# The feed-forward stage of a four-layer model: all remainders made by VectorE, another order of the first and last splits, and other PSUM banks for the last token tile

## The chip, the cores and the metric

The kernel runs on one core of one Trainium2 chip. The metric is the time of one execution in device microseconds. The kernel before took 2660.16 us (median of 3 runs, 2657.3 to 2661.0).

## The reference

The program computes two layers of one kind (attention, two recurrent mixers, a mixture of experts) and then two layers of a second kind. The change is in the last stage of the second kind, which runs twice, once in each of those two layers (sequence 512, D_MODEL 1024, D_FF 2816):

```python
x = x + mix @ w_out[l]

h2 = rms_norm(x, ffn_norm_g[l])
x = x + (jax.nn.silu(h2 @ w_gate[l]) * (h2 @ w_up[l])) @ w_down[l]
```

Everything is fp32.

## The kernel before

The whole stage is `out_ffn_stage`. It is called twice, with the same shapes.

**Products from parts.** TensorE multiplies fp32r values. Each operand is split into a rounded high part, written by ScalarE as a copy (`..._hi`), and a remainder `raw - hi`, written by VectorE or GpSimd as a subtraction (`..._lo`). `product` issues three matmuls for each tile: hi·hi, hi·lo, lo·hi (lines 233 to 235, in helper functions used everywhere).

**The output projection.** Four token tiles t of 128 rows; for each, two halves of 512 columns are summed in PSUM banks (`sum_bank`). VectorE adds them to x (`add`), ScalarE squares (`square`), VectorE normalises into `h` (`normalise`), and TensorE transposes `h` in eight blocks (`turn`, line 1956), four to each of two banks (`turn_bank`, banks 4 and 5). `turn(3)`, for the last tile, stands on TensorE behind the first two groups of the gate and up projections.

**Gate and up projection.** The product is done with seven half-size products P1 to P7 instead of eight (Strassen's scheme, in Winograd's form): for each of C = 11 chunks of 256 hidden columns, the seven products of `PRODUCTS` are *groups*, g = 0 to 76, each 24 matmuls of 256 columns. Groups 0 to 3 are P1 and P2 of chunks 0 and 1, 4 to 8 the rest of chunk 0, 9 to 13 the rest of chunk 1, and from 14 on seven for each chunk. The token operands (`x_operands`, names A11, A12, A22, S1 to S4) are made once: VectorE makes the sums S1 to S4 for the token tiles 2 and 3 (`make_sum`, lines 2172 to 2182), ScalarE their high parts (`split_sum`, line 2062; `split_a22`, line 2067), and GpSimd (line 2141) or VectorE (2187, 2192) the remainders. The weight operands are made for each group: VectorE makes the sums T3, T1, T2, T4 of a chunk (`make_w`, line 2214), ScalarE the high part (`w_split_hi`, line 1882), and `w_split_lo` (line 1888) the remainder. They lie in a ring of four places (RING = 4): the split of group g waits until group g - 4 has been multiplied.

**The order of work.** It is written out by hand, for each engine its own list; each engine goes through its list in order, and a semaphore holds it where an input or a place is not ready. In the middle, iteration g of ScalarE's and VectorE's loops does the split of group g and then `after(g - 4)`, which combines the products of a group into the hidden values: VectorE's lines 2223 to 2243, ScalarE's copy of P1 (2075) and its two Silus (2078 and 2081). A list `by_pool` says which engine makes a group's remainder: GpSimd for the first four groups and for P1, P7, P5 and P3, VectorE for P2, P6 and P4.

**Down projection.** The hidden values are split in eleven parts j (`hidden_split_hi`, line 2086; `hidden_split_lo`, line 1894). The high part of j overwrites token operands, so it waits for the last product that reads those (`hidden_free`). Twelve weight units of the down projection follow; the first (`ffn_down_hi`, `ffn_down_lo`) has places of its own, the others go through `weights_hi` and `weights_lo` (lines 208 and 222). A unit of the first half needs two hidden parts.

## Time and profile before

| | us |
|---|---|
| median of 3 runs | 2660.16 |
| profiled execution, its own time | 2654.06 |
| span of the profiled execution | 2651.9 |
| TensorE busy with matmuls | 2399.8 (90%) |
| VectorE busy | 1750.7 (66%) |
| ScalarE busy | 1313.7 (50%) |
| GpSimd busy | 906.0 (34%) |

Times in the trace are counted from the start of the span. The first run of the stage lies between 1506 and 1925 us, the second between 2229 and the end. A mean over the span says little about this stage: what counts is which wait of TensorE ends last at each place.

### The profile page before, as it was taken

The page shows a single profiled execution, that of the slowest core. Times are in us where ns is not written, and L with a number is a line of the kernel's source. Part 1 is how long each engine was busy: PE and PEld are TensorE (multiplying, and loading weights), DVE is VectorE, ACT ScalarE, POOL GpSimd, SP SyncE. Part 2 cuts the span into 40 slices and gives each one's busy share as a digit, 9 for nine tenths or more (in the row PEclk, how much of TensorE's full clock was granted, in tenths as well). Part 3 has the DMA queues.
Part 4 walks back from the last instruction along what each step waited for, and adds up shares of the span by engine and source line. Part 5 has one row for each costly group of instructions (what it writes and reads, how often), then busy time and mean ns, then how long its engine had stood idle before and what let it go on. Part 6 is the DMA issues. An engine that isn't in the chain of part 4 may idle for free. (4 is left out here: it accounts for less than half of the span.)

```text
span 2651.9 us, 37244 instructions
## 1 busy us (share of the span) xinstructions
PE 2399.8 (90%) x14216; PEld 2019.2 (76%) x14216; DVE 1750.7 (66%) x2637; ACT 1313.7 (50%) x2638; POOL 906.0 (34%) x447
## 2 busy tenths in 40 slices
PE   7999887977999887977998989998989989899989
PEld 7866676767866676767786779996877857899967
DVE  1855757863845757867698569884256984788832
ACT  3556616763546616755746644442157465444511
POOL 3401305762402205762350155551024401555510
PEclk9999888998999888998998999999999999999999
DMA  4200018973200108973220203322121202023211
GB/s 157 85 32 1 31 66 331 353 280 125 81 33 1 32 35 337 356 272 123 80 80 1 77 34 110 111 104 80 67 105 64 80 1 88 32 105 119 96 72 72
DMA packets 54992, 285.82 MB, mean 108 GB/s; under 512 B 13216, under 2 KB 13216, under 8 KB 28704
## 3 DMA queue, kind: packets, MB, share of 16 engines
q1 hardware_dynamic: 45600, 266.65, 27.5%
q0 software_dynamic: 9216, 16.80, 1.7%
q8 instruction: 114, 1.87, 0.3%
q14 instruction: 62, 0.51, 0.1%
HBM read 275.02 MB, written 25.17 MB: 113 GB/s over the span
## 5 line engine op out<-in xcount | busy, mean ns | idle before, releaser
L222 POOL TENSOR_TENSOR weights_lo<-weights_raw,weights_hi 128x2048 fp32r<-128x2048 f32 (+4 forms) x53 | 239.8, 4525 | 503.1 <-ACT weights_hi L208 335.7
L233 PE MATMUL ps<-x_operands,weights_hi 128*128 128x256 f32 x1232 | 351.9, 286 | 7.0 <-POOL weights_lo L1888 6.1
L234 PE MATMUL ps<-x_operands,weights_hi 128*128 128x256 f32 x1232 | 350.2, 284 | 0.0
L235 PE MATMUL ps<-x_operands,weights_lo 128*128 128x256 f32 x1232 | 347.6, 282 | 0.0
L208 ACT ACTIVATE weights_hi<-weights_raw 128x2048 fp32r<-128x2048 f32 (+5 forms) x86 | 147.9, 1722 | 306.3 <-PE ps L235 294.6
L233 PEld LDWEIGHTS ps<-x_operands,weights_hi 128*128 128x128 f32 x1232 | 233.1, 189 | 9.4 <-POOL weights_lo L1888 7.3
L235 PEld LDWEIGHTS ps<-x_operands,weights_lo 128*128 128x128 f32 x1232 | 236.0, 192 | 0.0
L234 PEld LDWEIGHTS ps<-x_operands,weights_hi 128*128 128x128 f32 x1232 | 233.5, 189 | 0.0
L233 PE MATMUL ps<-weights_hi,attn_ht_hi 128*128 128x512 f32 (+2 forms) x576 | 203.1, 353 | 8.3 <-DVE weights_lo L222 6.9
L235 PE MATMUL ps<-weights_hi,attn_ht_lo 128*128 128x512 f32 (+2 forms) x576 | 200.4, 348 | 0.0
L234 PE MATMUL ps<-weights_lo,attn_ht_hi 128*128 128x512 f32 (+2 forms) x576 | 200.0, 347 | 0.0
L222 DVE TENSOR_TENSOR weights_lo<-weights_raw,weights_hi 128x2048 fp32r<-128x2048 f32 (+3 forms) x33 | 65.0, 1973 | 188.6 <-ACT weights_hi L208 188.6
L233 PE MATMUL ps<-weights_hi,x_operands 128*128 128x512 f32 x384 | 155.2, 404 | 24.4 <-DVE weights_lo L222 18.1
L1882 ACT ACTIVATE weights_hi<-ffn_w_sums 128x1024 fp32r<-128x1024 f32 x66 | 69.9, 1059 | 191.4 <-DVE ffn_w_sums L2214 183.7
L1888 POOL TENSOR_TENSOR weights_lo<-weights_raw,weights_hi 128x1024 fp32r<-128x1024 f32 x50 | 128.2, 2566 | 82.3 <-ACT weights_hi L1882 82.0
L234 PE MATMUL ps<-weights_lo,x_operands 128*128 128x512 f32 x384 | 154.4, 402 | 0.0
L233 PE MATMUL ps<-weights_hi,xt_hi 128*128 128x480 f32 (+2 forms) x384 | 138.1, 360 | 6.1 <-DVE weights_lo L222 2.5
L235 PE MATMUL ps<-weights_hi,xt_lo 128*128 128x480 f32 (+2 forms) x384 | 135.3, 352 | 0.0
L234 PE MATMUL ps<-weights_lo,xt_hi 128*128 128x480 f32 (+2 forms) x384 | 134.9, 351 | 0.0
L233 PEld LDWEIGHTS ps<-weights_hi,attn_ht_hi 128*128 128x128 f32 x576 | 109.5, 190 | 31.7 <-issue 9.1
L235 PE MATMUL ps<-weights_hi,ffn_hidden_lo 128*128 128x512 f32 x320 | 126.9, 397 | 0.0
L235 PEld LDWEIGHTS ps<-weights_hi,attn_ht_lo 128*128 128x128 f32 x576 | 109.5, 190 | 12.7
(526 smaller groups left out, 6521.9 us busy)
## 6 DMA issues: line engine op xcount, KB each, us to landing
weights_raw<-in_stream SPq DMA_DIRECT2D x96, 1024.0 KB, 4.7
weights_raw<-in_expert_gu SPq DMA_DIRECT2D x34, 1024.0 KB, 9.1
expert_raw<-in_expert_gu SPq DMA_DIRECT2D x30, 1024.0 KB
expert_raw<-in_expert_down SPq DMA_DIRECT2D x18, 1024.0 KB, 8.0
weights_raw<-in_expert_down SPq DMA_DIRECT2D x14, 1024.0 KB
weights_raw<-in_stream SPq DMA_DIRECT2D x12, 960.0 KB, 4.6
ffn_raw<-in_stream SPq DMA_DIRECT2D x10, 1024.0 KB, 5.1
weights_raw<-in_stream SPq DMA_DIRECT2D x8, 700.0 KB, 9.9
```

What stands on the lines that cost most here:

```text
L208: self.nc.scalar.activation(self.split_tiles(u)[0][:, 0:n], self.env.raw[:, u % self.RAW, 0:n], ACT.Copy).then_inc(self.hi_ready, 1)
L222: eng.tensor_tensor(lo[:, 0:n], self.env.raw[:, u % self.RAW, 0:n], hi[:, 0:n].bitcast(F32), ALU.subtract).then_inc(self.lo_ready, 1)
L233: nc.tensor.matmul(out, a[0], b[0], start=start, stop=False, **more)
L234: nc.tensor.matmul(out, a[0], b[1], start=False, stop=False, **more)
L235: return nc.tensor.matmul(out, a[1], b[0], start=False, stop=stop, **more)
L1882: nc.scalar.activation(ring(g)[0], quarter(c, w_of[p]), ACT.Copy).then_inc(w_hi_done, 1)
L1888: eng.tensor_tensor(lo, quarter(c, w_of[p]), hi.bitcast(F32), ALU.subtract).then_inc(w_lo_pool if by_pool[g] else w_lo_dve, 1)
```

## The change

- `by_pool` is False for every group: VectorE (line 1891 in the new file) makes every weight remainder, and those of the token sums and of all hidden parts. GpSimd keeps only the four remainders of A11 and A12.
- The transposes of the last token tile go to banks 2 and 3 instead of 4 and 5 (`turn_bank(t, b)`), and the products take their banks from a table, `PRODUCT_BANKS`, instead of counting on from 6.
- VectorE makes the first T3, T1 and T2 behind `normalise(1)` instead of `normalise(2)`; the remainders of groups 0 to 3 stand before and just behind the last `add`.
- ScalarE splits all four first groups ahead of `square(3)`. The token parts are made in the order of a list, `TOKEN_PARTS`.
- The hidden parts are made in the order 0, 1, 6, 7, 8, 9, 4, 5, 2, 3, 10 (`HIDDEN_ORDER`). ScalarE makes ten high parts in one row behind the first down unit; VectorE puts two remainders ahead of each of the last `after` calls. Both engines put the second down unit ahead of hidden part 10.

```diff
+PRODUCT_BANKS = (6, 7, 0, 1, 4, 5, 2, 3)
+TOKEN_PARTS = (("S3", 2), ("S2", 2), ("A22", 2), ("S3", 3), ("S2", 3), ("S1", 2), ("S4", 2), ("S1", 3), ("S4", 3), ("A22", 3))
+HIDDEN_ORDER = (0, 1, 6, 7, 8, 9, 4, 5, 2, 3, 10)
...
-    by_pool = [g < RING or p in ("P1", "P7", "P5", "P3") for g, (_, p) in enumerate(order)]
+    by_pool = [False] * N
...
-        def turn_bank(b):
-            return ps[:, 4 + b, :].rearrange("p (k s) -> p k s", k=4)
+        def turn_bank(t, b):
+            return ps[:, (2 if t == T - 1 else 4) + b, :].rearrange("p (k s) -> p k s", k=4)
...
-            return ps[:, (at[c, p] + 6) % NBANK, :]
+            return ps[:, PRODUCT_BANKS[at[c, p] % NBANK], :]
...
@@ TensorE
-                        if t == 3:
-                            pe.wait_ge(s_made, s_at("S2" if b else "S3", 2))
-                            if b == 1:
-                                pe.wait_ge(s_hi, 5)
-                                pe.wait_ge(s_lo_dve, 1)
+                        if t == T - 1:
+                            pe.wait_ge(added, 2 * t + b + 1)
...
-                    if g < 6:
-                        pe.wait_ge(added, 6 if g < 4 else 8)
-                    elif g == 6:
-                        pe.wait_ge(s_made, s_at("S3", 3))
-                    elif g == 7:
-                        pe.wait_ge(s_made, s_at("S2", 3))
-                        pe.wait_ge(s_lo_dve, 6)
+                    if g < 4:
+                        pe.wait_ge(added, 6)
+                    elif g < NBANK:
+                        t = 2 + (g - 4) // 2
+                        pe.wait_ge(s_made, s_at("S2" if g % 2 else "S3", t))
+                        if g % 2:
+                            pe.wait_ge(s_lo, s_split("A22", t))
...
@@ ScalarE
-                w_split_hi(act, 0)
-                w_split_hi(act, 1)
+                for g in range(RING):
+                    w_split_hi(act, g)
                 square(3)
-                w_split_hi(act, 2)
                 split_sum("S3", 2)
                 split_sum("S2", 2)
-                w_split_hi(act, 3)
+                split_a22(2)
                 after(0)
+                w_split_hi(act, 4)
+                after(1)
+                w_split_hi(act, 5)
+                split_sum("S3", 3)
+                split_sum("S2", 3)
                 split_sum("S1", 2)
                 split_sum("S4", 2)
...
-                    after(g - RING)
                     if g == N:
...
                         stream.split_hi(act, down)
-                    if g >= N:
-                        for j in range(3 * (g - N), min(3 * (g - N) + 3, C - 1)):
+                        for j in HIDDEN_ORDER[:-1]:
                             hidden_split_hi(j)
-                hidden_split_hi(C - 1)
-                for u in range(down + 1, down + len(downs) + 2):
+                    after(g - RING)
+                stream.split_hi(act, down + 1)
+                hidden_split_hi(HIDDEN_ORDER[-1])
+                for u in range(down + 2, down + len(downs) + 2):
...
@@ VectorE
-                for m in ("T3", "T1", "T2"):
-                    make_w(0, m)
+                    if t == 1:
+                        for m in ("T3", "T1", "T2"):
+                            make_w(0, m)
                 add(3, 0)
+                for g in range(3):
+                    w_split_lo(v, g)
                 add(3, 1)
                 make_sum("S3", 2)
                 make_sum("S2", 2)
+                w_split_lo(v, 3)
                 normalise(3)
...
-                    after(g - RING)
                     if g == N:
...
                         stream.split_lo(v, down)
                     if g >= N:
-                        for j in range(3 * (g - N), min(3 * (g - N) + 3, C - 1)):
-                            if not hidden_by_pool[j]:
-                                hidden_split_lo(v, j)
-                if not hidden_by_pool[C - 1]:
-                    hidden_split_lo(v, C - 1)
+                        for j in HIDDEN_ORDER[2 * (g - N):2 * (g - N) + 2]:
+                            hidden_split_lo(v, j)
+                    after(g - RING)
+                for j in HIDDEN_ORDER[2 * RING:-1]:
+                    hidden_split_lo(v, j)
+                stream.split_lo(v, down + 1)
+                hidden_split_lo(v, HIDDEN_ORDER[-1])
```

Some lines of the new file are numbered otherwise than before: 1888 is 1891 (weight remainder), 1894 is 1897 (hidden remainder), 2172 to 2182 are 2156 to 2166 (token sums), 2187 and 2192 are 2172 (token remainders), 2214 is 2193 (weight sums), 2223 to 2243 are 2202 to 2222 (combining).

VectorE's order at the start of the stage, from the last token tile's sums to the weight remainder of group 5 (`ps` is PSUM, `ffn_sums` holds S1 to S4). Before:

```order
L2172 TENSOR_TENSOR ffn_sums<-ffn_parts,ps 128x512
L2176 TENSOR_TENSOR ffn_sums<-ps,ffn_sums 128x512
L2161 RECIPROCAL ffn_rs<-ffn_rs 128x1
L2164 SCALAR_TENSOR_TENSOR ffn_h<-x,ffn_rs,ffn_g 128x1024
L2179 TENSOR_TENSOR ffn_sums<-ffn_sums,ffn_parts 128x512
L2182 TENSOR_TENSOR ffn_sums<-ffn_a_15839,ffn_sums 128x512
L2192 TENSOR_TENSOR x_operands<-ps,x_operands 128x4x128
L2172 TENSOR_TENSOR ffn_sums<-ffn_parts,ps 128x512
L2176 TENSOR_TENSOR ffn_sums<-ps,ffn_sums 128x512
L2187 TENSOR_TENSOR x_operands<-ffn_sums,x_operands 128x4x128 x2
```

and now:

```order
L1891 TENSOR_TENSOR weights_lo<-weights_raw,weights_hi 128x1024
L2145 RECIPROCAL ffn_rs<-ffn_rs 128x1
L2148 SCALAR_TENSOR_TENSOR ffn_h<-x,ffn_rs,ffn_g 128x1024
L2163 TENSOR_TENSOR ffn_sums<-ffn_sums,ffn_parts 128x512
L2166 TENSOR_TENSOR ffn_sums<-ffn_a_15839,ffn_sums 128x512
L2172 TENSOR_TENSOR x_operands<-ffn_sums,x_operands 128x4x128 x2
L2172 TENSOR_TENSOR x_operands<-ps,x_operands 128x4x128
L2156 TENSOR_TENSOR ffn_sums<-ffn_parts,ps 128x512
L2160 TENSOR_TENSOR ffn_sums<-ps,ffn_sums 128x512
L1891 TENSOR_TENSOR weights_lo<-ffn_w_sums,weights_hi 128x1024
L2172 TENSOR_TENSOR x_operands<-ffn_sums,x_operands 128x4x128 x2
L1891 TENSOR_TENSOR weights_lo<-ffn_w_sums,weights_hi 128x1024
```

The remainders of the token sums and of groups 3, 4 and 5 now stand in VectorE's row, the one of A22 (`x_operands<-ps`) two places later.

VectorE's order at the end of the gate and up projection, from the first down unit on (`ffn_hidden_lo` are the hidden parts' remainders, the last rows the next down units). Before:

```order
L222 TENSOR_TENSOR ffn_down_lo<-weights_raw,ffn_down_hi 128x2048
L1894 TENSOR_TENSOR ffn_hidden_lo<-ffn_hidden,x_operands 128x1024 x2
L2232 TENSOR_TENSOR ffn_parts<-ffn_parts,ps 128x512
L2233 TENSOR_TENSOR ffn_parts<-ffn_parts,ps 128x512
L1894 TENSOR_TENSOR ffn_hidden_lo<-ffn_hidden,x_operands 128x1024
L2235 TENSOR_TENSOR ffn_hidden<-ffn_parts,ps 128x2x256
L1894 TENSOR_TENSOR ffn_hidden_lo<-ffn_hidden,x_operands 128x1024 x2
L2238 TENSOR_TENSOR ffn_parts<-ffn_parts,ps 128x512
L2241 TENSOR_TENSOR ffn_hidden<-ffn_hidden,ffn_parts 128x2x256
L2243 TENSOR_TENSOR ffn_hidden<-ffn_hidden,ffn_parts 128x2x256
L1894 TENSOR_TENSOR ffn_hidden_lo<-ffn_hidden,x_operands 128x1024
L222 TENSOR_TENSOR weights_lo<-weights_raw,weights_hi 128x2048 x4
```

and now, from the fourth row of it on:

```order
L2208 TENSOR_TENSOR ffn_parts<-ffn_parts,ps 128x512
L1897 TENSOR_TENSOR ffn_hidden_lo<-ffn_hidden,x_operands 128x1024 x2
L2211 TENSOR_TENSOR ffn_parts<-ffn_parts,ps 128x512
L2212 TENSOR_TENSOR ffn_parts<-ffn_parts,ps 128x512
L1897 TENSOR_TENSOR ffn_hidden_lo<-ffn_hidden,x_operands 128x1024 x2
L2214 TENSOR_TENSOR ffn_hidden<-ffn_parts,ps 128x2x256
L1897 TENSOR_TENSOR ffn_hidden_lo<-ffn_hidden,x_operands 128x1024 x2
L2217 TENSOR_TENSOR ffn_parts<-ffn_parts,ps 128x512
L2220 TENSOR_TENSOR ffn_hidden<-ffn_hidden,ffn_parts 128x2x256
L2222 TENSOR_TENSOR ffn_hidden<-ffn_hidden,ffn_parts 128x2x256
L1897 TENSOR_TENSOR ffn_hidden_lo<-ffn_hidden,x_operands 128x1024 x2
L222 TENSOR_TENSOR weights_lo<-weights_raw,weights_hi 128x2048
```

Eleven remainders instead of six stand in VectorE's row; two pairs of ten lie behind `after(75)` or later, and the second down unit now stands ahead of the eleventh.

## Rows read from the trace of the kernel before

**Rows 1.** Waits of TensorE, whole span: us in total, times, longest

```profile
PE ps L1956 <- DVE x_operands L2192: 9.2, 2, 4.6
...
PE ps L233 <- POOL weights_lo L1888: 6.1, 6, 1.9
```

**Rows 2.** Timeline of TensorE, start of the first stage: start, us, instruction, idle before

```profile
1556.27 0.36 PE L233 MATMUL ps<-x_operands,weights_hi 128*128 128x256 f32 x1 [0.30 <-PE ps L235]
...
1567.30 1.09 PE L1956 MATMUL ps<-consts,ffn_h 128*128 128x128 f32 x4 [4.61 <-DVE x_operands L2192]
1568.04 0.56 PE L233 MATMUL ps<-x_operands,weights_hi 128*128 128x256 f32 x1
...
1572.67 0.34 PE L233 MATMUL ps<-x_operands,weights_hi 128*128 128x256 f32 x1
...
1589.97 0.38 PE L233 MATMUL ps<-x_operands,weights_hi 128*128 128x256 f32 x1 [1.93 <-POOL weights_lo L1888]
...
1614.62 0.39 PE L233 MATMUL ps<-x_operands,weights_hi 128*128 128x256 f32 x1 [0.88 <-POOL weights_lo L1888]
```

**Rows 3.** Windows: us, busy us of PE, PEld, DVE, ACT, POOL, granted clock, DMA

```profile
1505.00:1510.00 5.00, 3.52 (x11) 2.89 (x12) 2.70 (x3) 3.48 (x2) 0.00 (x0) 0.79 0.86 313
...
1565.00:1570.00 5.00, 2.70 (x13) 2.73 (x14) 3.14 (x5) 3.08 (x6) 5.00 (x4) 0.60 0.00 0
```

**Rows 4.** Timeline of VectorE, start of the first stage

```profile
1559.64 2.89 DVE L2179 TENSOR_TENSOR ffn_sums<-ffn_sums,ffn_parts 128x512 f32<-128x512 f32 x1
...
1576.82 1.22 DVE L1888 TENSOR_TENSOR weights_lo<-ffn_w_sums,weights_hi 128x1024 fp32r<-128x1024 f32 x1
1577.96 0.68 DVE L2192 TENSOR_TENSOR x_operands<-ps,x_operands 128x512 fp32r<-128x512 f32 x1
1578.56 2.82 DVE L2214 TENSOR_TENSOR ffn_w_sums<-weights_raw,ffn_w_sums 128x1024 f32<-128x1024 f32 x1
```

**Rows 5.** Timeline of ScalarE at the first Silu of the first stage

```profile
1582.01 0.63 ACT L2078 ACTIVATE ffn_hidden<-ffn_hidden 128x512 f32<-128x512 f32 x1 [3.10 <-DVE ffn_hidden L2223]
1582.55 1.04 ACT L1882 ACTIVATE weights_hi<-ffn_w_sums 128x1024 fp32r<-128x1024 f32 x1
```

**Rows 6.** Timeline of VectorE, a late chunk and a weight sum of an early one

```profile
1619.27 1.21 DVE L2214 TENSOR_TENSOR ffn_w_sums<-weights_raw,ffn_w_sums 128x1024 f32<-128x1024 f32 x1
...
1778.30 1.21 DVE L2214 TENSOR_TENSOR ffn_w_sums<-weights_raw,ffn_w_sums 128x1024 f32<-128x1024 f32 x1
1780.69 1.23 DVE L1888 TENSOR_TENSOR weights_lo<-ffn_w_sums,weights_hi 128x1024 fp32r<-128x1024 f32 x1 [1.19 <-ACT weights_hi L1882]
```

**Rows 7.** Timeline of VectorE, end of the gate and up projection

```profile
1785.12 2.29 DVE L222 TENSOR_TENSOR ffn_down_lo<-weights_raw,ffn_down_hi 128x2048 fp32r<-128x2048 f32 x1 [1.29 <-ACT ffn_down_hi L208]
1787.33 6.78 DVE L1894 TENSOR_TENSOR ffn_hidden_lo<-ffn_hidden,x_operands 128x1024 fp32r<-128x1024 f32 x2
...
1809.04 4.49 DVE L222 TENSOR_TENSOR weights_lo<-weights_raw,weights_hi 128x2048 fp32r<-128x2048 f32 x2 [0.58 <-ACT weights_hi L208]
```

**Rows 8.** Timeline of GpSimd, same place

```profile
1786.96 16.14 POOL L1894 TENSOR_TENSOR ffn_hidden_lo<-ffn_hidden,x_operands 128x1024 fp32r<-128x1024 f32 x5 [2.78 <-ACT x_operands L2086]
```

**Rows 9.** Timeline of ScalarE, same place

```profile
1783.09 1.90 ACT L208 ACTIVATE ffn_down_hi<-weights_raw 128x2048 fp32r<-128x2048 f32 x1
1784.89 8.63 ACT L2086 ACTIVATE x_operands<-ffn_hidden 128x1024 fp32r<-128x1024 f32 x9
```

**Rows 10.** Timeline of TensorE, first and second down unit, first stage

```profile
1790.98 0.47 PE L233 MATMUL ps<-ffn_down_hi,x_operands 128*128 128x512 f32 x1 [0.42 <-DVE ffn_hidden_lo L1894]
...
1811.47 0.77 PE L233 MATMUL ps<-weights_hi,x_operands 128*128 128x512 f32 x1 [9.06 <-DVE weights_lo L222]
...
1815.31 0.39 PE L233 MATMUL ps<-weights_hi,x_operands 128*128 128x512 f32 x1
```

**Rows 11.** Timeline of TensorE, the same two places of the second stage

```profile
2290.90 1.09 PE L1956 MATMUL ps<-consts,ffn_h 128*128 128x128 f32 x4 [4.61 <-DVE x_operands L2192]
...
2535.09 0.77 PE L233 MATMUL ps<-weights_hi,x_operands 128*128 128x512 f32 x1 [9.07 <-DVE weights_lo L222]
```

More of the change, by code:

```diff
@@ L1732, in out_ffn_stage @@
     names = ("gains_loaded", "small_loaded", "summed", "added", "squared", "root_ready", "root_inverted", "normed", "turned",
[L1733 to L1735 removed]
+             "x_hi", "x_lo", "s_made", "s_hi", "s_lo", "w_made", "w_hi_done", "w_lo_dve", "w_lo_pool",
+             "p_done", "p1_kept", "gated_left", "gated_right", "combined", "hidden_done", "hidden_hi", "hidden_lo",
+             "stored", "tile_summed")
     (gains_loaded, small_loaded, summed, added, squared, root_ready, root_inverted, normed, turned, x_hi, x_lo, s_made, s_hi,
[L1737 to L1738 removed]
+     s_lo, w_made, w_hi_done, w_lo_dve, w_lo_pool, p_done, p1_kept, gated_left, gated_right, combined,
+     hidden_done, hidden_hi, hidden_lo, stored, tile_summed) = (env.sem(stage, n) for n in names)
     w_loaded = [env.sem(stage, f"w_loaded{s}") for s in range(4)]
@@ L1864, in hidden_free @@
             return at[C - 1, ("P1", "P5", "P6", "P7", "P2", "P4")[j // 2]] + 1
-        hidden_by_pool = [j % 2 == 1 for j in range(C)]
-        hidden_count = [sum(b == hidden_by_pool[j] for b in hidden_by_pool[:j + 1]) for j in range(C)]
         def hidden_wait(eng, j):
-            eng.wait_ge(hidden_lo_pool if hidden_by_pool[j] else hidden_lo_dve, hidden_count[j])
+            eng.wait_ge(hidden_lo, HIDDEN_ORDER.index(j) + 1)
         def w_split_hi(act, g):
@@ L1891, in hidden_split_lo @@
         def hidden_split_lo(eng, j):
-            eng.wait_ge(hidden_hi, j + 1)
+            eng.wait_ge(hidden_hi, HIDDEN_ORDER.index(j) + 1)
             hi, lo = hidden_pair(j)
-            eng.tensor_tensor(lo, hidden_all(j), hi.bitcast(F32), ALU.subtract
-                              ).then_inc(hidden_lo_pool if hidden_by_pool[j] else hidden_lo_dve, 1)
+            eng.tensor_tensor(lo, hidden_all(j), hi.bitcast(F32), ALU.subtract).then_inc(hidden_lo, 1)
         with nc.Block() as block:
@@ L2066, in split_a22 @@
                     act.wait_ge(summed, 2 * T)
-                    nc.scalar.activation(x_part("A22", 0, t), turn_bank(1), ACT.Copy).then_inc(s_hi, 1)
+                    nc.scalar.activation(x_part("A22", 0, t), turn_bank(t, 1), ACT.Copy).then_inc(s_hi, 1)
                 def after(m):
@@ L2136, in _ @@
                                                 ).then_inc(x_lo, 1)
-                for g in range(4):
-                    w_split_lo(nc.gpsimd, g)
-                for i, m in enumerate(SUMS):
-                    pool.wait_ge(s_hi, i + 1)
-                    nc.gpsimd.tensor_tensor(x_part(m, 1, 2), s_raw(m, 2), x_part(m, 0, 2).bitcast(F32), ALU.subtract
-                                            ).then_inc(s_lo_pool, 1)
-                for g in range(4, N):
+                for g in range(N):
                     if by_pool[g]:
                         w_split_lo(nc.gpsimd, g)
-                for j in range(C):
-                    if hidden_by_pool[j]:
-                        hidden_split_lo(nc.gpsimd, j)
             @block.vector
@@ L2171, in make_sum @@
                         dve.wait_ge(x_hi, 8)
-                        ins = v.tensor_tensor(s_raw(m, t), raw_part("A11", t), turn_bank(0), ALU.subtract)
+                        ins = v.tensor_tensor(s_raw(m, t), raw_part("A11", t), turn_bank(t, 0), ALU.subtract)
                     if m == "S2":
@@ L2259, in _ @@
                 make_sum("S4", 2)
-                rest_of_a22(2)
+                for m in ("S3", "S2", "A22"):
+                    rest_of(m, 2)
                 make_sum("S3", 3)
                 make_sum("S2", 3)
-                rest_of_sum("S3")
-                rest_of_sum("S2")
+                w_split_lo(v, 4)
+                rest_of("S3", 3)
+                rest_of("S2", 3)
+                w_split_lo(v, 5)
                 make_sum("S1", 3)
                 make_sum("S4", 3)
-                rest_of_sum("S1")
-                rest_of_sum("S4")
-                w_split_lo(v, 5)
-                rest_of_a22(3)
+                rest_of("S1", 2)
+                rest_of("S4", 2)
+                for m in ("S1", "S4", "A22"):
+                    rest_of(m, 3)
                 for g in range(6, N + RING):
```

41 lines of the change are left out of this document (12 added, 29 removed).

## The prediction, written before the changed kernel ran

> **What bounds the kernel now.** TensorE is the engine that sets the end (90% of the span), so I read its waits first, then its timeline where the longest lie, then the timelines of the engines it waits for. The stage's own waits come in equal pairs, one in each of its two runs [rows 1, 11]; what the first run shows counts twice.
>
> Places A (start). Groups 0 and 1 start at 1556.27 [rows 2]. The transposes of the last token tile then stop for 4.61 us, until VectorE has made the remainder of A22, because they use the same bank. Behind the stop the granted clock is 0.60 [rows 3], and the 22 matmuls from 1568.04 to 1572.67 take 0.21 us each [rows 2]. Later TensorE waits 1.93 us (group 8) and 0.88 us (group 16) for GpSimd's remainders. From group 16, at 1614.62, to the first down unit at 1790.98 with 0.42 us idle [rows 2, 10] there are 61 groups in 175.9 us: 2.88 us each, 24 matmuls of 0.12 us, with no gap that counts. From 1556.27 to 1614.62 are 58.35 us; 16 groups (46.1) and the eight transposes (0.8: the four behind the stop took 0.74 at the slow clock [rows 2], eight take as long at the full one) take 46.9. So 11.4 us are lost there.
>
> Place B (end). The first down unit runs from 1790.98 to 1811.47 - 9.06 = 1802.41. Then TensorE waits 9.06 us for the second unit's remainder. That stood in VectorE's row behind all its hidden remainders. The 9 matmuls from 1811.47 to 1815.31 take 0.43 us instead of 0.235 (11.43 us over 48), so the slow clock costs another 1.7 us [rows 10]. Lost: 9.06 + 0.42 + 1.7 = 11.2 us.
>
> **Prices.** Alone, VectorE's next instruction starts 1.14 us after a remainder of 1024 columns began (duration 1.22) and 0.60 us after one of 512 (0.68) [rows 4]. A sum of 512 with both inputs in SBUF took 2.89 us and a weight sum 2.82 us beside GpSimd [rows 4], hidden remainders 3.39 us on VectorE (6.78 for two) and 3.23 us on GpSimd (16.14 for five) [rows 7, 8]. Without GpSimd I take 1.14 for each. ScalarE: 1.04 for a weight high part, a Silu 0.63 [rows 5], 0.96 for a hidden high part (8.63 for nine) and 1.90 for a down unit [rows 9]. For a hand-over between engines I take 0.1.
>
> The contention agrees with the Trainium skill ("SBUF — State Buffer", "Who interferes with whom"): a VectorE instruction with two SBUF inputs and a GpSimd instruction that reads SBUF block each other. By that page no VectorE instruction is stretched after 1551, which is what the rows' short durations already say.
>
> **Place A after.** The transposes wait only for `add(3, ...)` and the normalised row, so they follow group 1 at 1562.1; the stop and the slow clock behind it go. Group 2 starts at 1562.9, and 3 to 9 would start at 1565.8, 1568.7, 1571.5, 1574.4, 1577.3, 1580.2, 1583.1. Moving T3, T1, T2 and four remainders ahead costs nothing: VectorE had those stretches free, waiting for TensorE's sums. Now VectorE. Before, its normalised row was done when the next row began at 1559.64 [rows 4]; one remainder (group 3) more stands ahead: 1560.8. From there to the end of group 6's remainder its row holds 16 instructions of 512 (2 + 3 + 2 + 2 + 2 + 2 + 3) and 4 of 1024 (remainders 4, 5, 6 and T4): 16 x 0.60 + 4 x 1.14 = 14.2, and 0.2 for two sums that wait for the one before: 1575.2. Group 4's remainder and S3's are ready by 1566.9, group 5's by 1568.6: in time. Group 6 starts at 1575.3, 0.9 late. Group 7's remainder hangs on a ring: VectorE's add of P2 (0.6), ScalarE's Silu (0.6) and high part (1.0), VectorE's remainder (1.2), 0.1 between them: 1578.8, 0.6 late. Group 8 has the same ring: 1582.3, 0.6 late. Then T3, T1, T2 of chunk 1 stand ahead of group 9's remainder, 3.4 + 1.2: 1586.9, 1.7 late. Groups 10 to 16 follow with 0.3 us lost at group 11 and 16: group 16 starts at 1586.9 + 7 x 2.88 + 0.3 = 1607.4. **Gain 1614.6 - 1607.4 = 7.2 us**, of the 11.4 that are lost now; 4.1 stay.
>
> **The middle.** Here nothing is gained and something may be lost. For each chunk VectorE's work is 11 instructions of 1024 columns (7 remainders, 4 sums) and 9 of 512: 11 x 1.14 + 9 x 0.60 = 17.9 us, with 0.5 for instructions that wait for the one before 18.4, and TensorE takes 7 x 2.88 = 20.2. It fits. Before, T4 of chunks 2 and 10 began at 1619.27 and 1778.30 [rows 6]: 19.9 us a chunk, because of the stretched instructions and of the 1.19 us between T4 and the remainder of P4. That wait is now covered by P5's remainder, which stands between them. The tightest place: at P2 of a chunk VectorE has one remainder, three sums, two adds and P7's remainder to do, 1.14 + 3.42 + 1.2 + 1.2 = 7.0 us, and it starts 1.1 us behind the product three groups back; P7 is wanted 11.5 us behind that. 3.4 us in hand.
>
> **Place B after.** I keep the old times of TensorE here (group 76 ends at 1790.6) and shift at the end. ScalarE began the down unit's high part at 1783.09 [rows 9], behind a Silu that waits for VectorE's add of P2. That add now comes 1.2 us sooner (the wait of [rows 6] is gone) and, an estimate, 0.7 more for the instructions ahead of it that GpSimd stretched. So the high part runs from 1781.2 to 1783.1. VectorE then goes without a pause: the unit 2.2, ten hidden remainders 11.4, `after(73)` to `after(76)` 1.3 + 1.2 + 0.6 + 1.9 = 5.0, the second unit 2.2: 1783.1 + 20.8 = 1803.9, with hand-over and tail 1804.2. ScalarE's ten high parts are done by 1792.7, always ahead. The first down unit still starts at 1790.6 (its two parts are ready at 1787.7) and ends at 1802.0. TensorE waits about 2.2 us instead of 9.06. All ten hidden parts are now wanted by the second unit (`HIDDEN_ORDER` puts 2 and 3 ninth and tenth); they lie ahead of the unit's remainder anyway, so that costs nothing. **Gain 1811.5 - 1804.2 = 7.3 us.**
>
> The slow clock there: idle 1.93 us between dense groups left no slow matmuls behind it (the eight groups from 1589.97 to 1614.62, less the 0.88, took 2.97 us each, where slow ones take 5) [rows 2]; 4.61 and 9.06 did, and the stretch with 3.1 us of idle at 1505 has 0.79 [rows 3]. 2.2 is nearest to 1.93, so I take the full clock, a further gain of 1.7; the other bound is 0.
>
> **Sum.** 7.2 + 7.3 + 1.7 = 16.2 a run, 32.4 for both. I take off 2 for hand-overs that I have not seen: 30. Against its own time the profiled execution would be 2654.06 - 30 = 2624. The median lies 6.1 above it; with the median 2660.2 - 30 = **2630**. What a measurement of this kernel can tell from no change is about 0.2%, 5 us.
>
> **Rivals.**
> 1. *VectorE becomes the bound of the middle.* The Trainium skill ("Perfetto Trace Analysis", "Optimizing Scalar/DVE Operations") says that with a saturated VectorE, offloading some work, even to GpSimd, may make sense; this change does the reverse. It also says ("VectorE: DVE Perf Modes", "The DRAIN you can't avoid") that the next instruction doesn't start until the pipeline is empty. By full durations, a chunk is 11 x 1.22 + 9 x 0.68 = 19.5 us, just under 20.2; the starts in [rows 4] lie closer than that. It loses once a chunk costs over 20.2. If half a chunk's waits (the 1.19 of [rows 6] and as much again) came on top of the 19.5, it is 21.9: (21.9 - 20.2) x 10 = 17 us a run, more than the 16 gained: 2662 or, with two more waits, 2680. From 21.8 us a chunk the kernel is slower. For it: each engine's list is in order, and VectorE has 2 us of slack per chunk. Against: the starts 1.14 and 0.60 apart, and the long lead. Chance 0.05.
> 2. *The gain at the start is mostly eaten* by the rings at groups 6 to 9 (each link 0.3 longer, and late weights for T3 of chunk 1 or 2): 3 instead of 7.2, 2630 + 8.4 = 2638. Chance 0.12.
> 3. *At place B the wait stays long*, over 5 us, since a hand-over breaks VectorE's unbroken row (`after(76)` waits for a Silu that waits for `after(75)`), and the clock falls too: 4 + 1.7 a run less, 2641. Chance 0.11.
> 4. *Nothing is gained*: other work was as late as what is moved. 2660. The rows name one releaser at each stop. Chance 0.03.
>
> **How the numbers follow.** The forecast has 0.69. Its own range is 2624 to 2636: the slow clock would add 3.4, hand-overs 2 to 3 either way. To hold eight in ten, with most of rivals 2 and 3 and a faster start below, the range is 2621 to 2642. Faster by over 0.2%: 0.69 + 0.12 + 0.11 = 0.92; within: 0.03 (rival 4) + 0.01 of rival 1; slower: the other 0.04 of rival 1.
>
> **What would show it.** In the changed profile: no stop at the transposes and no window of granted clock under 0.9 from 1556 to 1600; stops of 0.5 to 2 us at groups 6 to 9, now released by VectorE; group 16 near 1607; middle chunks of 20.2 us on TensorE; VectorE's weight remainders 1.22 us each; the second down unit after some 2 us of idle. The forecast is wrong if TensorE has repeated stops in chunks 3 to 10, or if the last stop is over 5 us.

## The result, and the profile after it

The changed kernel took 2628.34 us (median of four executions, 2623.89 to 2630.52), the kernel before in the same session 2660.58 (2657.3 to 2661.62). The ratio is 0.9879 with a 95% interval from 0.9862 to 0.9896: 1.2% faster. The profiled execution took 2628.48 us, its span is 2626.5 us.

The head of its page, with the busy time of each engine:

```profile
span 2626.5 us, 37236 instructions
...
PE 2401.4 (91%) x14216; PEld 2020.8 (77%) x14216; DVE 1755.6 (67%) x2747; ACT 1318.1 (50%) x2638; POOL 609.9 (23%) x337
```

GpSimd (POOL) has lost 110 instructions and 296 us, from 906.0 us and 447 instructions. VectorE (DVE) has gained those 110 instructions, and only 4.9 us of busy time (from 1750.7). Groups of VectorE's instructions by form in one stretch of the first stage, 1560 to 1820, show where they found room. The columns are count, busy us, mean ns and idle time. First the kernel before, at two lines that add 512 columns (L2241 has both inputs in SBUF, L2235 has one in PSUM) and one that sums weights:

```profile
L2241 DVE TENSOR_TENSOR ffn_hidden<-ffn_hidden,ffn_parts 128x512 f32<-128x512 f32 x11 | 25.3, 2302 | 0.4
...
L2214 DVE TENSOR_TENSOR ffn_w_sums<-weights_raw,ffn_w_sums 128x1024 f32<-128x1024 f32 x11 | 15.9, 1450 | 0.0
...
L2235 DVE TENSOR_TENSOR ffn_hidden<-ffn_parts,ps 128x512 f32<-128x512 f32 x11 | 7.5, 679 | 0.0
```

The same three after the change, where they stand at L2193 (weight sum), L2220 and L2214:

```profile
L2193 DVE TENSOR_TENSOR ffn_w_sums<-weights_raw,ffn_w_sums 128x1024 f32<-128x1024 f32 x11 | 13.4, 1217 | 0.0
...
L2220 DVE TENSOR_TENSOR ffn_hidden<-ffn_hidden,ffn_parts 128x512 f32<-128x512 f32 x11 | 7.6, 693 | 0.4
...
L2214 DVE TENSOR_TENSOR ffn_hidden<-ffn_parts,ps 128x512 f32<-128x512 f32 x11 | 7.5, 679 | 0.0
```

The sum with two SBUF inputs falls from 2302 to 693 ns, the one that reads PSUM stays at 679 in both. Before, ten of the eleven instructions of L2241 ran beside an instruction of GpSimd and took 2.43 to 2.60 us each, the eleventh ran without one and took 0.69. Ten of the eleven of L2235 ran beside GpSimd too and took 0.68 all the same. This is what the Trainium skill states ("SBUF — State Buffer", "Who interferes with whom"): a VectorE instruction with two SBUF inputs contends with a GpSimd instruction that reads SBUF, one with at most one SBUF input does not. Both traces agree with it.

TensorE's timeline at place A, with the idle time before an instruction and its releaser, answers to [rows 2]:

```profile
1556.16 0.36 PE L233 MATMUL ps<-x_operands,weights_hi 128*128 128x256 f32 x1 [0.30 <-PE ps L235]
...
1574.90 0.38 PE L233 MATMUL ps<-x_operands,weights_hi 128*128 128x256 f32 x1 [0.37 <-DVE weights_lo L1891]
...
1578.37 0.39 PE L233 MATMUL ps<-x_operands,weights_hi 128*128 128x256 f32 x1 [0.33 <-DVE weights_lo L1891]
...
1581.84 0.39 PE L233 MATMUL ps<-x_operands,weights_hi 128*128 128x256 f32 x1 [0.34 <-DVE weights_lo L1891]
...
1586.51 0.39 PE L233 MATMUL ps<-x_operands,weights_hi 128*128 128x256 f32 x1 [1.53 <-DVE weights_lo L1891]
```

The stop of 4.61 us at the transposes is gone. Four short ones are left, at groups 6 to 9, all for VectorE's remainders. From group 9 on there is none until the down product, so group 16 starts at 1586.51 + 7 x 2.88 = 1606.7 (1614.62 before).

VectorE's timeline at groups 7 and 8 shows the ring that makes them late. VectorE adds P2 into the hidden values, ScalarE's list has the Silu of that sum ahead of the next high part, and VectorE waits 1.65 us for this high part:

```profile
1574.77 0.68 DVE L2202 TENSOR_TENSOR ffn_hidden<-ffn_parts,ps 128x512 f32<-128x512 f32 x1
1577.09 1.23 DVE L1891 TENSOR_TENSOR weights_lo<-ffn_w_sums,weights_hi 128x1024 fp32r<-128x1024 f32 x1 [1.65 <-ACT weights_hi L1885]
1578.23 0.68 DVE L2202 TENSOR_TENSOR ffn_hidden<-ffn_parts,ps 128x512 f32<-128x512 f32 x1
1580.56 1.23 DVE L1891 TENSOR_TENSOR weights_lo<-weights_raw,weights_hi 128x1024 fp32r<-128x1024 f32 x1 [1.65 <-ACT weights_hi L1885]
```

TensorE at place B answers to [rows 10, 11]: the first matmul of the first down unit, and of the second in both stages:

```profile
1783.19 0.47 PE L233 MATMUL ps<-ffn_down_hi,x_operands 128*128 128x512 f32 x1 [0.41 <-DVE ffn_hidden_lo L1897]
...
1796.87 0.59 PE L233 MATMUL ps<-weights_hi,x_operands 128*128 128x512 f32 x1 [2.25 <-DVE weights_lo L222]
1797.25 0.63 PE L234 MATMUL ps<-weights_lo,x_operands 128*128 128x512 f32 x1
1797.68 0.63 PE L235 MATMUL ps<-weights_hi,ffn_hidden_lo 128*128 128x512 f32 x1
...
2509.76 0.47 PE L233 MATMUL ps<-weights_hi,x_operands 128*128 128x512 f32 x1 [1.90 <-DVE weights_lo L222]
```

The wait of 9.06 us is now 2.25 and 1.90 us. VectorE, which it waits for, has no pause from the down unit's remainder to the second unit's (first and last three of its rows; an x2 row has two instructions, 1.14 us apart):

```profile
1775.83 2.29 DVE L222 TENSOR_TENSOR ffn_down_lo<-weights_raw,ffn_down_hi 128x2048 fp32r<-128x2048 f32 x1 [1.82 <-ACT ffn_down_hi L208]
1778.04 2.35 DVE L1897 TENSOR_TENSOR ffn_hidden_lo<-ffn_hidden,x_operands 128x1024 fp32r<-128x1024 f32 x2
1780.31 0.68 DVE L2206 TENSOR_TENSOR ffn_parts<-ffn_parts,ps 128x512 f32<-128x512 f32 x1
...
1791.56 0.69 DVE L2222 TENSOR_TENSOR ffn_hidden<-ffn_hidden,ffn_parts 128x512 f32<-128x512 f32 x1
1792.16 2.35 DVE L1897 TENSOR_TENSOR ffn_hidden_lo<-ffn_hidden,x_operands 128x1024 fp32r<-128x1024 f32 x2
1794.44 2.29 DVE L222 TENSOR_TENSOR weights_lo<-weights_raw,weights_hi 128x2048 fp32r<-128x2048 f32 x1
```

Windows of the changed kernel: busy time of PE, PEld, DVE, ACT and POOL with their instructions, then granted clock, DMA share and GB/s. They are the start, the middle, and the first matmuls of the second down unit in both stages:

```profile
1556.00:1580.00 24.00, 23.14 (x189) 22.75 (x190) 21.02 (x29) 14.84 (x23) 0.00 (x0) 1.00 0.13 45
1640.00:1660.00 20.00, 20.00 (x169) 20.00 (x169) 18.74 (x21) 9.28 (x11) 0.00 (x0) 1.00 0.30 106
1797.00:1799.00 2.00, 2.00 (x6) 1.50 (x7) 2.00 (x2) 0.00 (x0) 0.00 (x0) 0.52 0.65 184
2512.00:2514.00 2.00, 2.00 (x7) 1.55 (x6) 0.95 (x1) 0.00 (x0) 0.00 (x0) 0.53 0.86 354
```

At the start the clock is full. Before, it was 0.60 in the window of [rows 3], which still has the end of the stop in it, and 0.50 from 1567.00 to 1572.00. At the second down unit it falls to the lower of its two levels in both stages, and 8 matmuls stand 0.43 us apart.

**Where the 25.4 us between the two profiled spans (2651.9 and 2626.5) lie.** Distances between TensorE's rows, first stage / second stage, from the start of group 0:

| | before | after | gain |
|---|---|---|---|
| to the first down unit | 234.71 / 234.72 | 227.03 / 227.02 | 7.7 / 7.7 |
| to the second down unit | 255.20 / 255.23 | 240.71 / 240.35 | 14.5 / 14.9 |
| from the first stage's second unit to group 0 of the second stage | 468.39 | 472.54 | -4.1 |

The stages gained 29.4 us. Between them, where the diff touches nothing but the end of the first stage, this execution lost 4.1. Windows over exactly this stretch, for the kernel before, the changed one, and the kernel of experiment 1, whose work there is that of before:

```profile
1811.47:2279.86 468.39, 439.79 (x2308) 356.07 (x2309) 270.87 (x474) 220.64 (x666) 100.38 (x41) 0.97 0.19 68
```

```profile
1796.87:2269.41 472.54, 445.91 (x2309) 361.20 (x2309) 273.63 (x478) 222.98 (x668) 94.90 (x39) 0.96 0.19 67
```

```profile
1813.87:2285.86 471.99, 445.67 (x2308) 360.84 (x2309) 271.11 (x474) 221.19 (x666) 100.13 (x41) 0.96 0.19 67
```

The granted clock is 0.96 for 0.97. The kernel of experiment 1 lost 3.6 us there by the same clock with nothing changed in its work, and over the 13 profiles of this case the stretch lasts from 465.7 us (clock 0.98) to 473.2 (0.96). So nothing shows the 4.1 as an effect of the change; the granted clock, which differs from execution to execution, accounts for as much. The profiled execution of the kernel before was also a quick one, 2654.06 against a median of 2660. Below, the distances inside the stages compare kernels: those of the two stages of one profile agree to 0.4 us, and "to the first" is 227.0 to 227.1 in four kernels that share this part. The medians are 32.2 apart.

### The profile page after: what moved, and what is told of

It is laid out like the page before. It is cut to its first block and busy times, and to the rows that moved or that the text cites. A ratio compares the mean times of both kernels' runs of the same rounds, so it can differ in the third digit from the quotient of the medians.

```text
span 2626.5 us, 37236 instructions
## 1 busy us (share of the span) xinstructions
PE 2401.4 (91%) x14216; PEld 2020.8 (77%) x14216; DVE 1755.6 (67%) x2747; ACT 1318.1 (50%) x2638; POOL 609.9 (23%) x337
## 5 line engine op out<-in xcount | busy, mean ns | idle before, releaser
L233 PE MATMUL ps<-x_operands,weights_hi 128*128 128x256 f32 x1232 | 347.9, 282 | 5.7 <-DVE weights_lo L1891 5.1
L234 PE MATMUL ps<-x_operands,weights_hi 128*128 128x256 f32 x1232 | 347.2, 282 | 0.0
L234 PEld LDWEIGHTS ps<-weights_lo,attn_ht_hi 128*128 128x128 f32 x576 | 110.8, 192 | 11.8
```

The lines of the kernel that those rows point to most:

```text
L233: nc.tensor.matmul(out, a[0], b[0], start=start, stop=False, **more)
L234: nc.tensor.matmul(out, a[0], b[1], start=False, stop=False, **more)
```

## The experiments

All kernels are edits of the changed one unless it is said. "To the first" and "to the second" mean the distances of the table above.

**1. Own banks alone, on the kernel before.** Theory: own banks don't remove work that is late, so the stop moves to the next group that needs it. Rival: the gain at the start is the banks'.

```diff
+PRODUCT_BANKS = (6, 7, 0, 1, 4, 5, 2, 3)
-            return ps[:, 4 + b, :].rearrange("p (k s) -> p k s", k=4)
+            return ps[:, (2 if t == T - 1 else 4) + b, :].rearrange("p (k s) -> p k s", k=4)
...
-                        if t == 3:
-                            pe.wait_ge(s_made, s_at("S2" if b else "S3", 2))
...
+                        if t == T - 1:
+                            pe.wait_ge(added, 2 * t + b + 1)
```

> The kernel before, with nothing but the banks of the change: the last tile's transposes in banks 2 and 3, the products by the new table. Theory A (the gain at the start comes from the order of VectorE's and ScalarE's lists and from GpSimd being out of it; the banks alone move the stop, they don't remove it): TensorE no longer stops 4.6 us at the transposes and keeps its full clock there, but stops 3 to 5 us at group 4 and again at 5, 7 and 8, since GpSimd's and VectorE's remainders come only 0.7 us sooner. Group 16 starts 0.5 to 1.5 us sooner than 1614.6, the whole 1 to 3 us faster, within noise. Rival B (the shared banks were the loss): stop and slow clock both go, 6 to 7 us a run of the stage, 12 to 14 us in all.

Measured: 2659.0 us against 2659.86, ratio 0.9997 (0.9987 to 1.0007). TensorE's timeline of this kernel, its stops in the first stage's first 60 us:

```profile
1575.98 0.58 PE L233 MATMUL ps<-x_operands,weights_hi 128*128 128x256 f32 x1 [4.58 <-POOL weights_lo L1889]
...
1592.38 0.39 PE L233 MATMUL ps<-x_operands,weights_hi 128*128 128x256 f32 x1 [1.94 <-POOL weights_lo L1889]
...
1617.02 0.39 PE L233 MATMUL ps<-x_operands,weights_hi 128*128 128x256 f32 x1 [0.89 <-POOL weights_lo L1889]
```

No stop at the transposes, and the same 4.6 us at group 4, behind them, with the lower clock behind it too (0.50 from 1576.00 to 1581.00). To the first: 234.6 (234.7). The banks alone are worth 0.1 us; 0.5 to 1.5 was expected.

**2. Banks as before, with the rest of the change.** The waits at the transposes and at groups 4 to 7 are then those of before.

```diff
-PRODUCT_BANKS = (6, 7, 0, 1, 4, 5, 2, 3)
+PRODUCT_BANKS = (6, 7, 0, 1, 2, 3, 4, 5)
-            return ps[:, (2 if t == T - 1 else 4) + b, :].rearrange("p (k s) -> p k s", k=4)
+            return ps[:, 4 + b, :].rearrange("p (k s) -> p k s", k=4)
```

> The changed kernel with the banks as before: the last tile's transposes in banks 4 and 5 again, so that their second half waits for the remainder of A22 of tile 2. Theory A: that remainder is now done at 1563.5, so the stop is about 1 us and most of it is taken up at group 6, which was 0.4 late anyway: group 16 comes 0.3 to 1 us later than 1606.7, 1 to 2 us over the changed kernel in all. Rival B: the stop comes back at 4 to 5 us with the slow clock, and 8 us or more of the 32 are lost.

Measured: 2624.54, ratio 0.9879 (0.9854 to 0.9903). TensorE's timeline of this kernel at the last tile's transposes:

```profile
1565.49 0.63 PE L1957 MATMUL ps<-consts,ffn_h 128*128 128x128 f32 x4 [1.07 <-DVE x_operands L2174]
```

A stop of 1.07 us comes back, and the stage is only 0.13 us longer (to the first 227.16): the next stops, which hang on VectorE, shrink by what this one takes. With experiment 1: the gain at the start is the engine's and the order's, not the banks'.

**3. Hidden remainders as before** (shared with GpSimd, not between the last sums, the second unit behind the hidden high parts).

```diff
+        hidden_by_pool = [j % 2 == 1 for j in range(C)]
...
-                    after(g - RING)
-                for j in HIDDEN_ORDER[2 * RING:-1]:
-                    hidden_split_lo(v, j)
-                stream.split_lo(v, down + 1)
```

> The changed kernel with the hidden parts as before: odd parts by GpSimd, the old order of parts, the second down unit last on both engines. Theory A (place B's gain comes from the hidden parts' order and from GpSimd being out of it): the stop ahead of the second down unit is 8 to 9 us again instead of 2.25, the start keeps its gain: 6 to 7 us a run, 12 to 15 us slower than the changed kernel. VectorE's hidden remainders take 3 us again. Rival B: the stop was long only because VectorE came late out of the middle; it is then about 5 us, and 5 to 6 us in all are lost.

Measured: 2642.61, ratio 0.9933 (0.9911 to 0.9955). TensorE's and then VectorE's timeline of this kernel:

```profile
1805.52 0.77 PE L233 MATMUL ps<-weights_hi,x_operands 128*128 128x512 f32 x1 [7.25 <-DVE weights_lo L222]
```

```profile
1781.36 6.79 DVE L1900 TENSOR_TENSOR ffn_hidden_lo<-ffn_hidden,x_operands 128x1024 fp32r<-128x1024 f32 x2
...
1792.03 6.21 DVE L1900 TENSOR_TENSOR ffn_hidden_lo<-ffn_hidden,x_operands 128x1024 fp32r<-128x1024 f32 x2
```

The wait is 7.25 us, where 8 to 9 was expected. VectorE's hidden remainders cost 3.1 to 3.4 us each again in these four (1.14 without GpSimd); a fifth takes 2.24. To the first 227.1, to the second 245.7: 5.0 and 5.4 us more than after the change. So of the 7 us that place B gained, 5 come from this part. The run changes the engine and the order together. An estimate from VectorE's rows: the five remainders take 15.2 us here and ten without GpSimd 11.4, so some 3.8 of the 5 are the engine, and the rest is the order. Experiment 4 has 1.1 to 1.5 of the rest: they came with the weights' remainders.

**4. GpSimd in the middle again** (remainders of P1, P7, P5 and P3 from group 14 on).

```diff
-    by_pool = [False] * N
+    by_pool = [g >= 14 and p in ("P1", "P7", "P5", "P3") for g, (_, p) in enumerate(order)]
```

> The changed kernel with GpSimd making the weight remainders of P1, P7, P5 and P3 again, from group 14 (chunk 2) on; the start and the hidden parts stay as in the change. Theory A (TensorE bounds the middle with either engine): no stops in chunks 3 to 10 and 2.88 us a group, at most one stop under 1 us at group 16. But VectorE leaves the last chunk some 2 us later, since GpSimd stretches its instructions, so the stop ahead of the second down unit grows from 2.25 to about 4: 2 to 3 us a run, 4 to 6 us slower than the changed kernel. Rival B: the middle part of the change is where the gain comes from, and 10 us or more are lost. Rival C: nothing changes, under 1 us.

Measured: 2633.15, ratio 0.9907 (0.9885 to 0.9928). TensorE's timeline of this kernel at group 13 and at the second down unit:

```profile
1598.71 0.38 PE L233 MATMUL ps<-x_operands,weights_hi 128*128 128x256 f32 x1 [0.97 <-DVE weights_lo L1891]
...
1798.51 0.47 PE L233 MATMUL ps<-weights_hi,x_operands 128*128 128x512 f32 x1 [3.38 <-DVE weights_lo L222]
```

VectorE's remainder for group 13, beside GpSimd's first one of the middle (1594.90, 2.67 us), takes 3.42 us instead of 1.22:

```profile
1595.23 3.42 DVE L1891 TENSOR_TENSOR weights_lo<-ffn_raw,weights_hi 128x1024 fp32r<-128x1024 f32 x1
```

To the second 243.1: 2.4 and 2.7 us more a stage, half of it the stop at group 13 and half a longer last stop. The middle's move pays at its two ends, not inside it.

**5 to 7. More load on VectorE in the middle: one, two or three remainders a chunk made twice**, in chunks 2 to 10, with a wait of the engine for the first of the two. The value is the same both times. Rival 1 of the prediction is tried here: where does VectorE become the bound, and what does one of its instructions cost?

```diff
+MORE = ('P3',)          # two_more: ('P4', 'P3'); three_more: ('P1', 'P4', 'P3')
...
+            if c >= 2 and p in MORE:
+                eng.tensor_tensor(lo, quarter(c, w_of[p]), hi.bitcast(F32), ALU.subtract).then_inc(repeated, 1)
+                eng.wait_ge(repeated, (c - 2) * len(MORE) + MORE.index(p) + 1)
```

> The changed kernel with one more instruction of VectorE in each chunk from 2 to 10: P3's weight remainder is made twice. It costs 1.14 us and about 0.1 for the wait between the two. Theory A (a chunk costs VectorE 18.4 us by the distances between starts): 19.7 us a chunk against 20.2 of TensorE, so no stop in the middle, at most 1 us a run of the stage. Rival (a chunk costs its full durations and waits, 20.0 us, as the rule on the drain has it): 21.3 us a chunk, 1.1 us lost in each of nine chunks, 10 us a run, 20 in all.

> The same with two more (P4's and P3's remainders made twice). Theory A: 20.9 us a chunk, 0.7 over TensorE: small stops in every chunk, 5 to 7 us a run, and a later start of the last chain by 2 to 3 us: 15 to 20 us in all over the changed kernel. Rival: 22.7 us a chunk, 45 us in all.

> The same with three more (P1's, P4's and P3's). Theory A: 22.2 us a chunk, 2.0 over TensorE: 18 us a run in the middle and 3 at the end, some 40 us in all, so slower than the kernel before. Rival: 24.1 us a chunk, 70 us in all.

Measured:

| | ratio (95%) | us (executions) | to the first | stops in the middle |
|---|---|---|---|---|
| one more | 0.9887 (0.9865 to 0.9909) | 2630.6 (2) | 227.0 | none |
| two more | 0.9955 (0.9936 to 0.9974) | 2648.95 (3) | 235.4 | 0.32 a chunk |
| three more | 1.0036 (1.0025 to 1.0046) | 2670.02 (8) | 246.8 | 1.59 a chunk |

TensorE's timeline of the kernel with three more, the stops of three chunks in a row, and then VectorE's with a remainder made twice:

```profile
1674.05 0.39 PE L233 MATMUL ps<-x_operands,weights_hi 128*128 128x256 f32 x1 [1.59 <-DVE weights_lo L1895]
...
1696.23 0.39 PE L233 MATMUL ps<-x_operands,weights_hi 128*128 128x256 f32 x1 [1.59 <-DVE weights_lo L1895]
...
1718.41 0.39 PE L233 MATMUL ps<-x_operands,weights_hi 128*128 128x256 f32 x1 [1.59 <-DVE weights_lo L1895]
```

```profile
1702.16 1.23 DVE L1893 TENSOR_TENSOR weights_lo<-ffn_w_sums,weights_hi 128x1024 fp32r<-128x1024 f32 x1
1703.42 1.23 DVE L1895 TENSOR_TENSOR weights_lo<-ffn_w_sums,weights_hi 128x1024 fp32r<-128x1024 f32 x1
```

A chunk lasts 22.18 us with three more and 20.91 with two (from 1633.47 to 1654.38). In both VectorE's row has no pause over such a chunk, so VectorE is what bounds it. A repeat costs 1.26 with its wait. 22.18 - 3 x 1.26 = 18.4 and 20.91 - 2 x 1.26 = 18.4: VectorE's price for a chunk, the prediction's number. With one more it is 19.7, under TensorE's 20.2, and nothing stops. The kernel with three more is slower than the kernel before, as rival 1 says, at 22.2 us a chunk. The Trainium skill ("VectorE: DVE Perf Modes", "The DRAIN you can't avoid") says that the next instruction does not start until the pipeline is empty, and in the same place that an instruction that is not held starts earlier. Full durations would make 19.5 us of a chunk; the runs are 1.1 us below that, so here most instructions go by the exception.

**8. The second down unit sooner**: it waits for seven hidden parts instead of ten, and its remainder stands ahead of the last four.

```diff
-HIDDEN_ORDER = (0, 1, 6, 7, 8, 9, 4, 5, 2, 3, 10)
+HIDDEN_ORDER = (0, 1, 6, 7, 2, 3, 8, 9, 4, 5, 10)
...
-                        for j in HIDDEN_ORDER[2 * (g - N):2 * (g - N) + 2]:
+                        for j in HIDDEN_ORDER[2 * (g - N):2 * (g - N) + 2][:2 if g < N + 3 else 0]:
...
-                for j in HIDDEN_ORDER[2 * RING:-1]:
-                    hidden_split_lo(v, j)
                 stream.split_lo(v, down + 1)
-                hidden_split_lo(v, HIDDEN_ORDER[-1])
+                for j in HIDDEN_ORDER[6:]:
+                    hidden_split_lo(v, j)
```

> The changed kernel with the hidden parts in the order 0, 1, 6, 7, 2, 3, 8, 9, 4, 5, 10 and the second down unit's remainder behind the first six, ahead of the other five. Theory A (place B is VectorE's unbroken row, and the slow clock follows the stop): four remainders of 1.14 us leave the row ahead of the unit, 4.6 us against a stop of 2.25: the stop goes but for 0.4 us, and with it the 1.7 us of slow clock: 3.5 to 4 us a run, 7 to 8 us in all faster than the changed kernel. Rival B: the stop goes and the slow clock comes anyway: 4 us in all. Rival C: the third unit waits in its place for parts 4 and 5: no gain.

Measured: 2620.1, ratio 0.9847 (0.9831 to 0.9864). TensorE has no stop at the second unit, and no slow clock behind it. To the second 238.3 in both stages: 2.4 and 2.0 less. The full clock behind it comes on top: from the second stage's second unit to the end of the span are 115.1 us instead of 116.7. Together that is the 3.5 to 4 us a stage of theory A.

**9. High parts of groups 6 to 8 sooner on ScalarE**, ahead of the two Silus that wait for VectorE. This opens the ring at groups 7 and 8.

```diff
-                for g in range(6, N + RING):
+                for g in range(6, 9):
+                    w_split_hi(act, g)
+                for g in range(6, 9):
+                    after(g - RING)
+                for g in range(9, N + RING):
```

> The changed kernel with ScalarE's high parts of groups 6, 7 and 8 in one row, ahead of the Silus of chunks 0 and 1. Theory A (the stops at groups 7, 8 and 9 are the ring add, Silu, high part, remainder, in which VectorE idles 1.65 us twice): VectorE's row to group 9 becomes unbroken and is some 3 us sooner; the stops of 0.33, 0.34 and 1.53 us go, that of 0.37 at group 6 stays: 2.2 us a run, 4 to 5 us in all faster than the changed kernel. Rival: the stop moves on to groups 10 to 16, since VectorE's work up to chunk 2 is the same, and half or more of it is given back.

Measured: 2620.6, ratio 0.9855 (0.984 to 0.987). Only the stop at group 6 is left (0.33). To the first 223.9: 3.2 less for stops whose idle time was 0.33 + 0.34 + 1.53 = 2.2.

**10. Both, 8 and 9 together.**

> The changed kernel with both edits, the hidden order 0, 1, 6, 7, 2, 3, 8, 9, 4, 5, 10 with the second unit ahead of five parts, and the early high parts. The two places are 200 us apart and share no buffer, so the gains add: 3.5 to 4 and 2.2 us a run, 11 to 13 us faster than the changed kernel, 2616 or so. Rival: VectorE's lead at the end of the middle does not depend on the start, so nothing is added beyond either; a sum smaller by more than 2 us would show a link between the places.

Measured: 2615.15 (2609.4 to 2616.48, five executions) against 2658.65, ratio 0.9832 (0.9818 to 0.9845): the fastest version found. To the second 235.2, 5.5 and 5.2 less than after the change, which is the sum of what the two edits gave there alone (2.4 and 2.0, and 3.2 and 3.1). TensorE's timeline of this kernel from group 0 to the second down unit of the first stage has two stops, and the window over the start of the second unit has the full clock:

```profile
1579.08 0.39 PE L233 MATMUL ps<-x_operands,weights_hi 128*128 128x256 f32 x1 [0.38 <-DVE weights_lo L1891]
...
1784.22 0.47 PE L233 MATMUL ps<-ffn_down_hi,x_operands 128*128 128x512 f32 x1 [0.41 <-DVE ffn_hidden_lo L1897]
```

```profile
1795.00:1800.00 5.00, 5.00 (x23) 4.05 (x22) 5.00 (x6) 1.92 (x1) 0.00 (x0) 1.00 0.54 198
```

**11. GpSimd at the start again** (remainders of groups 0 to 3, and of P1, P7, P5 and P3 before group 14), with the new order of VectorE's work.

```diff
-    by_pool = [False] * N
+    by_pool = [g < 14 and (g < RING or p in ("P1", "P7", "P5", "P3")) for g, (_, p) in enumerate(order)]
...
-                for g in range(3):
-                    w_split_lo(v, g)
...
-                w_split_lo(v, 3)
...
-                w_split_lo(v, 4)
```

> The changed kernel with GpSimd making the weight remainders of groups 0 to 3 and of P1, P7, P5 and P3 in chunks 0 and 1 again, all else as in the change (the order of both lists, the banks, the token remainders by VectorE). It tells the order's share of the 7.7 us at the start from the engine's. Theory A (the engine counts: a GpSimd remainder takes 2.4 to 3.4 us against 1.2, and stretches VectorE's sums): no stop at the transposes, but stops of 1.5 to 3 us at groups 8 and 9 and one under 1 us at 7; the first down unit starts 2 to 4 us later than 227.0 us behind group 0: 4 to 8 us slower than the changed kernel in all. Rival (the new order alone brings it): under 1 us a run.

Measured: 2633.64, ratio 0.9899 (0.988 to 0.9918). TensorE's timeline of this kernel, its stops at groups 6, 7 and 8:

```profile
1576.85 0.39 PE L233 MATMUL ps<-x_operands,weights_hi 128*128 128x256 f32 x1 [1.62 <-POOL weights_lo L1891]
...
1581.40 0.39 PE L233 MATMUL ps<-x_operands,weights_hi 128*128 128x256 f32 x1 [1.42 <-DVE weights_lo L1891]
...
1586.48 0.39 PE L233 MATMUL ps<-x_operands,weights_hi 128*128 128x256 f32 x1 [1.93 <-POOL weights_lo L1891]
```

GpSimd's and then VectorE's timeline at the first of them:

```profile
1574.34 2.45 POOL L1891 TENSOR_TENSOR weights_lo<-weights_raw,weights_hi 128x1024 fp32r<-128x1024 f32 x1 [9.65 <-ACT weights_hi L1885]
```

```profile
1575.09 2.78 DVE L2193 TENSOR_TENSOR ffn_w_sums<-weights_raw,ffn_w_sums 128x1024 f32<-128x1024 f32 x1
```

The two instructions lie over each other. VectorE's weight sum takes 2.78 us instead of 1.22, and the remainder costs GpSimd 2.45 us where VectorE makes one in 1.22. To the first 229.6: 2.6 more. So of the 7.7 us gained there, 2.6 are the engine of the weights' remainders, and 5.1 the order of the work with the token remainders on VectorE. Which of these two it is was not tried.

## Why the prediction was right, and what was off in it

The forecast was 2630 and the median is 2628.34, inside the range. The mechanism was right at both places, and that the two numbers are as near as this is in part luck, as the sum below shows. The steps one by one, for one stage:

- **Place A**, 7.2 predicted, 7.7 measured to the first down unit. The stops were forecast at groups 6 to 9, 0.9, 0.6, 0.6 and 1.7 late. From the distances of the starts they cost 0.66 (group 6: 1574.90 against 1556.16 + 6 x 2.88 + 0.8), 0.59, 0.59 and 1.79, released by VectorE as said. Only the 0.3 for groups 11 and 16 did not come. The price of VectorE's row (1.14 and 0.60 apart) and the ring over ScalarE were right; experiment 9 opened that ring and its stops went, which confirms it.
- **The middle**, 0 predicted, and no stop in groups 10 to 76. 18.4 us a chunk is what experiments 6 and 7 measured. Rival 1 is real, but only from 1.8 us more a chunk on.
- **Place B**, 7.3 predicted, 6.8 and 7.2 measured (14.5 and 14.9 less 7.7). The stop was forecast at 2.2 and is 2.25 and 1.90. VectorE's row from the first down unit's remainder to the end of the second's was forecast at 20.8 us and takes 20.9 (1775.83 to 1794.44 + 2.29). The 0.42 us at the first unit were to go and stayed at 0.41: a stop of 0.41 to 0.50 stands ahead of the first unit in every kernel here but those with two and three more, which stop 2.7 us there; the releaser named is another each time (VectorE's hidden remainder, TensorE itself, an add), and what holds TensorE there is open.
- **The clock**, 1.7 predicted, 0 measured in the profiled execution. This is the step that failed: "2.2 is nearest to 1.93, so I take the full clock". The clock fell in both stages, and 8 matmuls at 0.43 instead of 0.235 cost 1.6 us each time. The other bound, 0, was on record. The runs show that within this range the length of the stop does not decide it: behind the twelve stops of 1.90 to 2.28 us at this place in seven kernels (after, shared banks, one more, two more, three more, early high parts, GpSimd at the start) it fell six times and stayed full six times; behind the three of 3.38 to 3.63 and all longer ones it fell. Experiment 8 takes the stop away, and the slow matmuls with it.
- **The sum**: the stages gave 29.4 against 29.0 without the clock. The 3.4 for the clock did not come and the 2 taken off for hand-overs were not needed, so two errors of opposite sign stood in the 30. What the medians have beyond the 29.4 (32.2) lies within what single executions vary by (6.6 us between the four).
- **Readings of the rows.** Three were not exact, and none changes the sum. The window of 0.60 in [rows 3] starts inside the stop; behind it the clock is 0.50. [rows 3] do not show the 3.1 us of idle near 1505; the trace has 3.12 at 1506.48. And 11.43 us over 48 matmuls are 0.238 each; 0.235 is the spacing in a dense stretch.
- **Rivals 2 to 4** did not happen, but for the fall of the clock in rival 3. The change does two separable things with their own gains, and neither is the banks.

## What to carry to other kernels

When GpSimd shares elementwise work with VectorE, price both engines before and after: here 110 subtractions moved onto the busier engine cost it 4.9 us in all, since its other instructions shrank. Before a stop is blamed on the resource that it names (a bank), look for the work that is late behind it; with own banks the same 4.6 us only moved on. Before work goes onto an engine with slack, find how far the slack reaches with a doubled instruction: here one more a chunk was free and three more lost everything.
